# Two RMSNorms applied to a product's output instead of its input, on one Trainium2 core

## The reference

```python
def rmsnorm(x, g):
    y = x * lax.rsqrt(jnp.mean(x * x, axis=-1, keepdims=True) + EPS)
    return y * g
...
def swiglu(h, w_gu, w_dn):
    gu = h @ w_gu
    return (jax.nn.silu(gu[..., :D_FF]) * gu[..., D_FF:]) @ w_dn
...
# layer 0: y = silu(layernorm(conv(...))), mo = memory attention
x = x + jnp.concatenate([mix, mo], axis=-1) @ w_o
x = x + swiglu(rmsnorm(x, g2), w_gu, w_dn)
# layer 1
z = rmsnorm(x, norm1) @ fox_w_in      # q, k, v, forget gate, memory q
q = rmsnorm(q_heads, g_q); k = rmsnorm(k_heads, g_k)
```

## Time and profile before

| | |
|---|---|
| median of 3 runs | 1964.14 us (1961.77 to 1972.73) |
| the profiled execution | 1962.56 us, of which its span 1960.9 us |
| PE busy | 1747.5 us (89%) |
| DVE, ACT, POOL busy | 860.3 us (44%), 568.0 us (29%), 129.0 us (7%) |
| mean granted PE clock | 0.951 of full speed |
| HBM traffic | 119 GB/s over the span |

### The profile page before, as it was taken

One profiled execution on the slowest core, in us unless ns is written; L12 is line 12 of the kernel. 1 busy time (PEld: TensorE's weight loads), 2 busy tenths in 40 slices (PEclk: granted clock), 3 DMA queues, 4 the chain that ended last, 5 costly groups with the idle time before them and its releaser, 6 DMA issues. The chain is left out here.

```text
span 1960.9 us, 34562 instructions
## 1 busy us (share of the span) xinstructions
PE 1747.5 (89%) x13565; PEld 1525.1 (78%) x13565; DVE 860.3 (44%) x1270; ACT 568.0 (29%) x935; POOL 129.0 (7%) x249
## 2 busy tenths in 40 slices
PE   6799968999999998999765788888878999999997
PEld 4687748999999998889634555555457999999997
DVE  3764554432333223675363666666525333232222
ACT  3444242322222121554121333333313222222110
POOL 3100100000000001444101000000000000000000
PEclk9899989999999999999787999999979999999999
DMA  4445512222223222223425699998741222223321
GB/s 134 139 119 141 146 44 65 67 84 86 85 75 95 81 76 59 60 70 82 154 87 147 198 317 309 298 314 281 241 154 54 86 83 78 85 75 91 89 77 59
DMA packets 247241, 244.40 MB, mean 125 GB/s; under 512 B 14523, under 2 KB 201997, under 8 KB 246367
## 3 DMA queue, kind: packets, MB, share of 16 engines
q1 hardware_dynamic: 235120, 213.58, 35.6%
q0 software_dynamic: 10896, 25.88, 4.9%
q10 hardware_dynamic: 1118, 3.53, 0.6%
HBM read 223.85 MB, written 8.61 MB: 119 GB/s over the span
## 5 line engine op out<-in xcount | busy, mean ns | idle before, releaser
L1530 PE MATMUL ps<-aH,wH 128*128 128x288 f32 x2224 | 487.8, 301 | 43.1 <-DVE aL L464 25.3
L1530 PE MATMUL ps<-aH,wL 128*128 128x288 f32 x2224 | 479.7, 297 | 0.0
L1530 PE MATMUL ps<-aL,wH 128*128 128x288 f32 x2224 | 479.4, 298 | 0.0
L1530 PEld LDWEIGHTS ps<-aH,wH 128*128 128x128 f32 x2224 | 361.3, 191 | 55.4 <-issue 39.2
L1530 PEld LDWEIGHTS ps<-aL,wH 128*128 128x128 f32 x2224 | 361.9, 191 | 0.0
L1530 PEld LDWEIGHTS ps<-aH,wL 128*128 128x128 f32 x2224 | 361.8, 190 | 0.0
L441 DVE TENSOR_TENSOR wL<-raw,wH 128x1024 fp32r<-128x1024 f32 (+1 forms) x171 | 223.4, 1307 | 312.4 <-ACT wH L1079 310.0
L1079 ACT ACTIVATE wH<-raw 128x1024 fp32r<-128x1024 f32 (+1 forms) x171 | 190.3, 1113 | 365.0 <-PE ps L1530 343.8
L1976 PEld LDWEIGHTS ps<-ident,kring 128*128 128x128 f32 x768 | 85.2, 145 | 96.7 <-issue 40.0
L1976 PE MATMUL ps<-ident,kring 128*128 128x128 f32 x768 | 117.8, 290 | 44.3 <-DVE kT L921 26.4
L1530 PE MATMUL ps<-gH,wH 128*128 128x288 f32 x704 | 151.6, 296 | 4.8 <-DVE gL L644 4.8
(11 more groups left out here) (346 smaller groups left out, 1681.5 us busy)
## 6 DMA issues: line engine op xcount, KB each, us to landing
kring<-in_cache_fox_k_dram SPq DMA_DIRECT2D x128, 384.0 KB, 4.3
vring<-in_cache_fox_v_dram SPq DMA_DIRECT2D x128, 384.0 KB, 4.4
raw<-in_w_gate_up_dram SPq DMA_DIRECT2D x88, 512.0 KB, 3.7
raw<-in_w_down_dram SPq DMA_DIRECT2D x32, 704.0 KB, 4.6
raw<-in_fox_w_in_dram SPq DMA_DIRECT2D x21, 512.0 KB, 3.8
shifted<-u_all SPq DMA_DIRECT2D x88, 106.5 KB, 2.2
raw<-in_w_out_dram SPq DMA_DIRECT2D x16, 512.0 KB, 4.2
raw<-in_conv_w_in_dram SPq DMA_DIRECT2D x14, 512.0 KB, 4.5
```

What stands on the lines that cost most here:

```text
L1530: mm = nc.tensor.matmul(ps[:, 2 * slot + h, 0:HT], weights[:, w], a[:, k0 + k, h * HT:(h + 1) * HT], start=(first and k == 0 and weights i ...
```

## The change

Norm 1 (ahead of layer 0's FFN) and norm 2 (ahead of the FoX input) no longer make a normalised tile. In `residual` with r = 1 or 2, as soon as `xT[j]` is new, ACT makes `aH[j]` = xT[j]·gain (its own scale operand) and DVE `aL[j]` = xT[j]·gain − aH[j] in one instruction; the products that follow start from these. `sum_squares` stands after the first product. `inverse_root` is the root on ACT and the reciprocal on DVE, into `rb` for the FFN and a new buffer `rn` for the FoX input; every product of the stage is multiplied by it as it leaves PSUM: in the FFN the gate (new `sq`, then Silu in place) and the up product (new `tmp`, then times `sq`), in the FoX input each tile by `rooted` on DVE, which takes the place of ACT's copy. ACT's `head_square` reads that `tmp`; the v tiles are no longer squared. `hi` and `lo` stand one chunk earlier in ACT's and DVE's order there. DVE's clears of `work` and `lfd`, which wait for `consts1`, keep their place behind DN0's residual, where norm 2 no longer stands between.

Since `aH`, `aL` are now written while w_o still reads the mixer's output, that output has buffers of its own, `mixH` and `mixL`, and `mixed_product` reads them, the memory's two tiles first. ACT's two copies of the memory's output stand right ahead of the LayerNorm's squares and no longer among the convolution's last copies; DVE's two subtractions stand behind the mean's.

```diff
+        mixH, o = at("mixH", [P, KD, T], BASE, F32R)
+        assert o <= yc_at
+        mixL, o = at("mixL", [P, KD, T], startup_end, F32R)
...
+            def inverse_root(r, factor):
+                dve.wait_ge(norm_root, r + 1)
+                link(nc.vector.reciprocal(factor[:], factor[:]))
...
+                    if r in (1, 2):
+                        gain = (V_N1, V_N2)[r % 2] + (r // 2) * KD + j0
+                        dve.wait_ge(vH_done, KD * r + j0 + 1)
+                        nc.vector.scalar_tensor_tensor(out=aL[:, j0], in0=xT[:, j0], scalar=vec[:, gain:gain + 1], in1=aH[:, j0].bitcast(F32),
+                                                       op0=ALU.mult, op1=ALU.subtract).then_inc(a_ready, 1)
...
+                    if l == 0:
+                        if f0 == 0:
+                            inverse_root(1, rb)
+                        dve.wait_ge(w_used, c0 + 2 * f0 + 1 + 4 * i)
+                        if f0 >= 2:
+                            dve.wait_ge(g_done, f0 - 1 + 2 * i)
+                        nc.vector.tensor_tensor(halves(sq[:, f0 % 2]), acc(2 * (f0 % 2)), halves(rb[:]), ALU.mult).then_inc(gr_done, 1)
+                        dve.wait_ge(w_used, c0 + 2 * f0 + 2 + 4 * i)
+                        if f0 >= 2:
+                            dve.wait_ge(gL_done, f0 - 1 + 2 * i)
+                        nc.vector.tensor_tensor(halves(tmp[:, f0 % 2]), acc(2 * (f0 % 2) + 1), halves(rb[:]), ALU.mult).then_inc(ur_done, 1)
+                        dve.wait_ge(ur_done, f0 + 1 + 2 * i)
+                        dve.wait_ge(silu_done, f0 + 1 + 2 * i)
+                        nc.vector.tensor_tensor(tmp[:, f0 % 2], tmp[:, f0 % 2], sq[:, f0 % 2], ALU.mult).then_inc(g_done, 1)
...
             residual(C_WO0, 1, 1)
-            norm(1)
             dve.wait_ge(stored, 16 * marks["layer 0 stored"])
             ffn(0)
             residual(C_DN0, 2, 2)
-            norm(2)
 
 
             dve.wait_ge(consts1, CONSTS1)
             link(nc.vector.memset(work[:, 0], 0.0))
             link(nc.vector.memset(lfd[:], 0.0))
             Z = MP
+
+            def rooted(z0, i=0, rows=P):
+
+                dve.wait_ge(w_used, C_FOX - Z + z0 + 1 + 2 * i)
+                if z0 >= Z + 2:
+                    dve.wait_ge(hn_done, z0 - 1 + 2 * i)
+                nc.vector.tensor_tensor(halves(tmp[0:rows, z0 % 2]), acc(z0 % 2)[0:rows], halves(rn[0:rows]), ALU.mult).then_inc(zr_done, 1)
...
             lo(C_FOX + 1)
             lo(C_FOX + 2)
+            inverse_root(2, rn)
+            rooted(Z, rows=NH)
+            rooted(Z + 1)
+            lo(C_FOX + 3)
...
-                lo(C_FOX - Z + z0 + 2, i)
+                rooted(z0 + 1, i)
+                lo(C_FOX - Z + z0 + 3, i)
...
+            def inverse_root(r, factor):
+                act.wait_ge(ss_ready, r + 1)
+                nc.scalar.activation(halves(factor[:]), ps[:, 4:6, 0:HT], ACT.Sqrt, bias=eps[:, 0:1]).then_inc(norm_root, 1)
...
+            def head_square(z0, i=0):
+                act.wait_ge(zr_done, z0 - MP + 1 + 2 * i)
+                act.wait_ge(hn_ready, z0 - 1 + 2 * i)
+                nc.scalar.activation(sq[:, z0 % 2], tmp[:, z0 % 2], ACT.Square).then_inc(z_done, 1)
...
+                    if r in (1, 2):
+                        gain = (V_N1, V_N2)[r % 2] + (r // 2) * KD + j0
+                        act.wait_ge(x_new, KD * (r - 1) + j0 + 1)
+                        nc.scalar.activation(aH[:, j0], xT[:, j0], ACT.Copy, scale=vec[:, gain:gain + 1]).then_inc(vH_done, 1)
...
+                        act.wait_ge(gr_done, f0 + 1 + 2 * i)
+                        nc.scalar.activation(sq[:, f0 % 2], sq[:, f0 % 2], ACT.Silu).then_inc(silu_done, 1)
...
-            for hp in range(MP):
-                nc.scalar.activation(aH[:, KC + hp], mb0["qm"][:, hp], ACT.Copy).then_inc(mo_hi, 1)
...
+            act.wait_ge(usc_done, 1)
+            for hp in range(MP):
+                nc.scalar.activation(mixH[:, hp], mb0["qm"][:, hp], ACT.Copy).then_inc(mo_hi, 1)
...
+                        if l == 0 and ready is not None and s == 0:
+                            sum_squares(1)
                 tile(0, ready=(a_ready, KD * (2 * l + 1)))
+                pe.wait_ge(norm_root, 2 * l + 2)
                 tile(1)
...
             def tile(z0, i=0, ready=None):
-                pe.wait_ge(z_done, z0 - 1 + 2 * i)
+                if z0 >= Z + 2:
+                    pe.wait_ge(zr_done, z0 - Z - 1 + 2 * i)
                 product(C_FOX - Z + z0, i, z0 % 2, aH, aL, 0, KD, True, True, ready)
             tile(Z, ready=(a_ready, KD * 2))
+            sum_squares(2)
             tile(Z + 1)
+            pe.wait_ge(norm_root, 3)
             pe.wait_ge(z_done, Z + 1)
```

More of the change, by code:

```diff
@@ L621, in tile @@
                         nc.vector.tensor_tensor(rb[:], rb[:], sq[:, (j0 - 1) % 2], ALU.add).then_inc(sq_added, 1)
+                if r in (1, 2):
+                    for j in range(KD):
+                        tile(j, 0)
+                    return
                 for j in range(2):
@@ L1216, in tile @@
                     hi(c0 + 2 * f0 + 2, 2 * i)
-                    if g0 + f0 >= 2:
+                    if l == 0:
+                        if f0 == 0:
+                            inverse_root(1, rb)
+                        act.wait_ge(gr_done, f0 + 1 + 2 * i)
+                        nc.scalar.activation(sq[:, f0 % 2], sq[:, f0 % 2], ACT.Silu).then_inc(silu_done, 1)
+                    else:
                         act.wait_ge(g_done, g0 + f0 - 1 + 2 * i)
-                    nc.scalar.activation(halves(sq[:, f0 % 2]), acc(2 * (f0 % 2)), ACT.Silu).then_inc(silu_done, 1)
+                        nc.scalar.activation(halves(sq[:, f0 % 2]), acc(2 * (f0 % 2)), ACT.Silu).then_inc(silu_done, 1)
                     act.wait_ge(g_done, g0 + f0 + 1 + 2 * i)
@@ L1389, in head_pass @@
             def head_pass(z0, i=0):
-                if z0 - Z + 1 < N_FOX:
-                    hi(z0 - Z + C_FOX + 1, i)
-                head_tile(z0, i)
+                if z0 - Z + 2 <= N_FOX:
+                    hi(z0 - Z + C_FOX + 2, i)
+                head_square(z0, i)
                 head_norm(z0 - 1, i)
-            with act.Fori(0, HP) as i:
+            with act.Fori(0, HP - 1) as i:
                 for z in range(2):
                     head_pass(Z + 2 + z, i)
-            for n in range(2 * HP + 2, N_FOX):
-                if n - 1 <= 3 * HP:
-                    hi(C_FOX + n + 1)
-                    head_tile(Z + n)
-                else:
-                    head_pass(Z + n)
+            head_pass(Z + 2 * HP)
+            for n in range(2 * HP + 1, 3 * HP + 1):
+                hi(C_FOX + n + 2)
+                if n == 2 * HP + 1:
+                    head_norm(Z + n - 1)
+            for n in range(3 * HP + 1, N_FOX):
+                head_square(Z + n)
+                if n - 1 > 3 * HP:
+                    head_norm(Z + n - 1)
             head_norm(Z + N_FOX - 1)
@@ L1533, in product, with mixed_product @@
                 mm.then_inc(w_used, 1)
+            def mixed_product(n0, i, slot, ready=False):
+                s = n0 % 2
+                pe.wait_ge(lo_done, n0 + 1 + 2 * i)
+                for n in range(KD):
+                    k = (KC + n) % KD
+                    if ready:
+                        pe.wait_ge(*((mo_lo, n + 1) if n < MP else (stage_done, n - MP + 1)))
+                    for weights, acts in ((wH[s], (mixH, mixL)), (wL[s], (mixH,))):
+                        for a in acts:
+                            for h in range(2):
+                                mm = nc.tensor.matmul(ps[:, 2 * slot + h, 0:HT], weights[:, k * P:(k + 1) * P], a[:, n, h * HT:(h + 1) * HT],
+                                                      start=(n == 0 and weights is wH[s] and a is mixH),
+                                                      stop=(n == KD - 1 and weights is wL[s]))
+                mm.then_inc(w_used, 1)
             def sum_squares(r):
@@ L1548, in tile @@
                     H_, L_ = (aH, aL) if per_tile == 1 else (gH, gL)
+                    if r == 1:
+                        mixed_product(c0 + j0, i, j0 % 2, ready is not None)
+                        return
                     for s in range(per_tile):
```

60 lines of the change are left out of this document (33 added, 27 removed).

## The result

The changed kernel took 1948.81 us in the median of 9 runs against 1964.14, a ratio of 0.9921 (95% interval 0.9892 to 0.9949). So it is faster by some 1%, as forecast. The first measurement, 15.3 us, falls short of the 21.1 of the sum; the second, 24.8 by its ratio and 30.3 by the medians, goes beyond it. The profiled execution's span fell from 1960.9 to 1944.3 us.

The account below looks back on a forecast made before the run. PE, busy 89%, bounds the kernel, so time comes only from its gaps: 0.6 − 13.7 + 0.8 − 12.0 + 0.7 + 1.5 + 0.5 + 0.5 = −21.1 from 1962.56, giving 1941.5 us. Forecast 1939 to 1946 (0.66), wider range 1936 to 1950.

Parts of the forecast that it names:

- What bounds: Whole kernel: PE busy 89% of the span, so time can only come out of PE's gaps; both norms wholly on the path.
- Norm 1: Between w_o and layer 0's FFN: up product starts 8.6 us after w_o instead of 22.3, so −13.7.
- The FFN: Layer 0's 22 tiles: added DVE work hidden, slack 2.5 falling to 1.7; only the wait ahead of DN0 grows, +0.8.
- Norm 2: DN0's end to the third FoX product: tile Z + 1 starts at +10.9, third product at about +17.9, so −12.0.
- the clock's +0.7: Behind norm 2's 2.3 us gap: PE's clock may fall to half rate; bounds 0 and 1.5, middle +0.7.
- The rule on the shared interfaces: Norm 2's place: GpSimd contends with vector instructions reading two SBUF inputs, so POOL's constants end up to 0.8 us later.
- Heads: q and k heads: weight copy ahead of the square adds 0.4 us per table pass, +1.5 in all, bounds 0 and 5.
- The sum +2.0: Heads of q and k: +1.5 for the table passes and +0.5 for the memory's q.
- k stores: v and k stores: stores and page loads come closer together, +0.5, bounds 0 and 5.
- the rival of the row loads: "Only norm 1 gains": POOL's row loads hang on DN0's end, norm 2's 12 us are lost, 1953; chance 0.05.
- LayerNorm: LayerNorm stage: ACT's two copies ahead of the squares delay them up to 1.26 us, part given back; +0.6.
- half eaten: Rival: FoX input's heads and stores at their bounds of 5 each, clock 1.5, gain 12.3, to 1950; chance 0.14.

Follow-up runs that it names:

- the second: The changed kernel, unedited, timed again in 6 runs against the kernel before: 1941.63 us against 1971.91, ratio 0.9874 (0.9833 to 0.9916).
- e1: Norm 1 alone moved behind its product, norm 2 and the FoX input as in the kernel before: ratio 0.9963 (0.9936 to 0.9991) against that kernel.
- e6: Changed kernel with two, then four more multiplications by rb per layer 0 FFN tile: stage 1.5 us, then 38.3 us longer; one timed execution each.
- e3: Changed kernel with DVE's two clears and their wait for POOL's constants behind the third weight split: ratio 0.9922 (0.9896 to 0.9948).
- e5: Changed kernel with ACT's weight copy and DVE's split at the heads put last again: first to last head sum 151.28 us for 144.91.
- e7: Changed kernel with ACT's two copies of the memory's output behind the LayerNorm's squares: mean's sums to last w_o tile 74.27 us, 1.6 less.

## Why the prediction was right, and where its sizes were off

- **What bounds** was right: PE's gaps at the norms were the whole gain. **Norm 1** gained 14.3, forecast 13.7: the up product starts 8.0 us behind w_o and not 8.6, since the sum of squares took 1.7 us (340.52 to 342.24) and not 2.2. e1 shows it alone.
- **The FFN** hid its added work as worked out, slack 1.8 for 1.7; e6 shows that it is slack and not load that counts. The gap ahead of DN0 grew to 3.15, forecast 3.2.
- **Norm 2**: tile Z + 1 at 10.9, exact; the clock's +0.7 was mis-sized. It cost 1.7 (8.1 us for 6.4), a little over the upper bound of 1.5, and not only sometimes: all nine profiles with this wait have 18.8 to 19.0 us in the stage, and the two without it 15.0.
- **The rule on the shared interfaces** (Trainium skill, "GPSIMD Engine Reference", "1. Specifications"): the trace agrees that the two engines contend, but the forecast's 0.8 did not come. POOL's constants ended 8.7 us after DN0 (773.31 − 764.57), 8.8 before. The kernel before had a vector instruction with two SBUF inputs there too, in its timeline:

```profile
775.28 0.75 DVE L621 TENSOR_TENSOR rb<-rb,sq 128x576 f32<-128x576 f32 x1
...
775.56 1.26 POOL L2325 TENSOR_SCALAR_AFFINE_SELECT win<-win 128x896 f32<-128x896 f32 x1
```

  Beside it POOL's first select took 1.26 us; in the changed kernel, where that addition comes later, it took 0.94, and the select at 767.49 now took 0.43, where its like in the kernel before took 0.19. So POOL lost some 0.3 us in both kernels. DVE lost a little too: the subtraction took 0.90 us for 0.82 at 335.93, where POOL is idle. What held the loss down is that DVE then waits for POOL: in e3, where its splits run on, the constants came 1.9 us later.
- **Heads**: +0.4 per wait came out as a number (0.36), but whether by the weight copy, as argued, is open after e5. The sum +2.0 was too high, 0.7 measured: PE's waits for `qkT` are five and no longer six, since the last pass loads no table and waits no more, and the passes without a wait are 0.1 shorter.
- **k stores**: +0.5 was too small, 1.6 to 2.6. The step that failed was the argument that POOL's 19.40 idle us would cover a shift of 12: they stood behind the v stores, which were the ones held back. It is the rival of the row loads, in a small form: a chain on POOL that hangs on DN0's end and does not move with PE.
- **LayerNorm**: +0.9 for +0.6, removed by e7.
- The sum of these, −19.7, is 1.4 from the forecast, and in part by luck: the heads, 1.3 too dear in the forecast, made up for the k stores, 1.1 to 2.1 too cheap. By its number alone the first measurement, 1948.81, lies beside the forecast's 1939 to 1946, where the forecast had put "half eaten"; the stages show that this is not what happened. The other 4 us of it are within its interval and about what the attention stage differs by between equal kernels. What decides there which execution gets the lower clock stays open.

## What to carry to other kernels

A norm whose factor is one per token can be applied behind the product: on a kernel bound by the matrix engine that takes everything but the sum of squares off the path, as long as the chain in the steady state keeps slack. When a stage disappears, look at what it had covered: a wait for constants and a store queue came to light here, and a wait at the end of a loop, there before, grew. By stage each could be had back by moving a few lines (3.9, 1.6 and, over both layers, 5.9 us), the first of them in full only together with the store queue. Where executions of one kernel differ by 20 us, compare stages between the same instructions, not times.
